# The next head's weights: raw copies in sixteen places instead of eight, their split spread over other slots, and three low parts of eight on GpSimd

## The reference

```python
u = rmsnorm(x, norm_g) @ w_in            # 1024 -> 4096 columns: qa ka va za | qr fr ir zr
# group A, 4 heads: differential attention with a distance bias
scores = einsum(q, k) * SCALE - slope * |q_pos - k_pos|, masked by chunks of 64
a  = softmax(scores[0]) - lam * softmax(scores[1]);  oa = a @ v
# group B, 4 heads: gated linear recurrence over time
state = exp(sum log_f) * state + k^T v;  orec = decayed scores @ v + q exp(cum) @ state
mix = concat(rmsnorm(oa) * silu(za), rmsnorm(orec) * silu(zr))
y   = rmsnorm(x + mix @ w_out, final_g)
# outputs: y, new keys and values, the new states, for both groups
```

## Time and profile before

| | |
|---|---|
| time, median of 3 runs | 1556.78 us (1556.17 to 1558.73) |
| time of the profiled execution | 1557.17 us |
| its span, first to last instruction | 1555.2 us |
| mean granted TensorE clock | 0.992 |
| TensorE, matmuls | 1502.5 us busy (97%) |
| TensorE, weight loads | 1286.8 us (83%) |
| VectorE | 933.1 us (60%) |
| ScalarE | 859.2 us (55%) |
| GpSimd | 678.5 us (44%) |
| chain that ended last | TensorE 84%, VectorE 6%, issue 4%, ScalarE 2%, GpSimd 2% |

### The profile page before, as it was taken

How to read it: one execution, slowest core, us unless ns; L and a number is a source line. 1 busy time by engine, 2 the same in 40 slices (tenths; PEclk the granted TensorE clock), 3 DMA queues, 4 the chain that set the end, 5 groups by cost and what they waited for, 6 DMA issues and landing times.

```text
span 1555.2 us, 25554 instructions
## 1 busy us (share of the span) xinstructions
PE 1502.5 (97%) x8432; PEld 1286.8 (83%) x8432; DVE 933.1 (60%) x2088; ACT 859.2 (55%) x2326; POOL 678.5 (44%) x1407
## 2 busy tenths in 40 slices
PE   5999999998999999989999999989999999899997
PEld 4788888887888888878888888878888888788886
DVE  6676666677555666685556656765656666732232
ACT  5666666756556555665555555755565655621121
POOL 6665555437554444355644444356444334400000
PEclk9999999999999999999999999999999999999999
DMA  7233222243522221133322221234222120434332
GB/s 232 87 128 114 95 79 79 79 146 101 156 72 96 68 68 45 62 119 111 101 90 69 68 69 46 85 97 138 94 68 72 65 69 15 155 127 145 138 121 67
DMA packets 99432, 149.13 MB, mean 96 GB/s; under 512 B 10288, under 2 KB 79792, under 8 KB 90608
## 3 DMA queue, kind: packets, MB, share of 16 engines
q1 hardware_dynamic: 99312, 147.62, 29.2%
HBM read 103.03 MB, written 44.56 MB: 95 GB/s over the span
## 4 chain that ended last, share of the span: by engine, by line
PE 84%; DVE 6%; issue 4%; ACT 2%; POOL 2%; SPq 1%; DMA 1%; DVEq 0%; POOLq 0%; ACTq 0%
PE pab L569 42%; PE oar L641 7%; PE qkb L694 7%; PE qkb L595 6%; PE pab L758 6%; PE qkb L758 6%; PE tb L632 3%; DVE scores L1151 3%; PE tb L673 2%; SPq L305 1%; PE oar L611 1%; PE oar L608 1%; PE tb L533 1%; PE tb L745 1%; PE oar L610 1%
## 5 line engine op out<-in xcount | busy, mean ns | idle before, releaser
L569 PE MATMUL pab<-w_hi,xr 128*128 128x512 f32 x2176 | 783.7, 403 | 5.5 <-DVE w_lo L1030 3.0
L569 PEld LDWEIGHTS pab<-w_hi,xr 128*128 128x128 f32 x2176 | 411.8, 189 | 87.0 <-ACT w_hi L811 4.5
L569 PE MATMUL pab<-w_lo,xr 128*128 128x512 f32 x1088 | 426.7, 392 | 0.0
L1372 POOL TENSOR_TENSOR dd<-dd 128x64 f32<-128x64 f32 x340 | 119.9, 353 | 457.0 <-DVE dd L1136 457.0
L569 PEld LDWEIGHTS pab<-w_lo,xr 128*128 128x128 f32 x1088 | 206.7, 190 | 32.8
L694 PE MATMUL qkb<-kp,q 128*128 128x512 f32 (+3 forms) x656 | 185.1, 364 | 1.8 <-DVE mxs L1151 1.6
L1151 DVE CUSTOM_DVE_ANT_0 scores<-qkb,bias 128x512 f32<-128x512 f32 (+4 forms) x136 | 84.7, 625 | 145.5 <-PE qkb L694 145.4
L914 ACT ACTIVATE scores<-scores,nmx 128x128 f32<-128x128 f32 (+16 forms) x136 | 156.9, 1165 | 19.0 <-DVE nmx L1161 19.0
L859 ACT ACTIVATE fb<-pab 128x256 f32<-128x256 f32 x68 | 26.1, 384 | 255.5 <-PE pab L569 255.5
L641 PE MATMUL oar<-vv,at 128*128 128x128 f32 x1104 | 151.8, 277 | 1.9 <-ACT at L880 1.9
L1106 DVE TENSOR_TENSOR q<-tb,q 128x256 fp32r<-128x256 f32 x68 | 28.9, 425 | 203.4 <-ACT kp L901 203.2
(11 more groups left out here) (151 smaller groups left out, 2624.1 us busy)
## 6 DMA issues: line engine op xcount, KB each, us to landing
xr<-xs SPq DMA_DIRECT2D x51, 1024.0 KB, 5.3
xs<-xr SPq DMA_DIRECT2D x17, 1024.0 KB, 3.9
w_raw<-in_w_in SPq DMA_DIRECT2D x48, 256.0 KB, 5.8
mix<-mx SPq DMA_DIRECT2D x68, 128.0 KB, 2.2
xr<-mix SPq DMA_DIRECT2D x17, 512.0 KB, 5.0
w_raw<-in_x_prompt SPq DMA_DIRECT2D x16, 512.0 KB, 3.9
scores<-in_x_prompt SPq DMA_DIRECT2D x16, 512.0 KB, 4.2
out<-vv SPq DMA_DIRECT2D x16, 512.0 KB, 3.0
```

What stands on the lines that cost most here:

```text
L569: last = mm(pab[:, b, :], x, w[:, kt, 512 * b:512 * b + 512], start=(kt == 0 and part == 0 and w is w_hi), stop=(kt == KT - 1 and part == 1))
L1372: g.tensor_tensor(o[:, :, 0, :], ref, c[:, :, 0, :], sub)
```

## The change

- `w_raw` gets 16 places, one for each piece. The raw weights of `b = 0` of the next head are loaded in slot 5, those of `b = 1` as before; `raw_behind` is gone. The smaller scratch area of the last hunk makes room for it.
- ScalarE splits pieces 0 to 5 of `b = 1` ahead of the last slot's `recurrence_columns`, and 6 and 7 right behind them. The places where pieces of `b = 1` stood now hold pieces 0 to 5 of `b = 0`, and 6 and 7 stand behind `gate_sigmoids`.
- GpSimd makes three low parts of eight in each half, 2, 4 and 6; of `b = 1` it makes two ahead of `exponents`. VectorE makes five instead of six. This also holds for the first head's weights at the start of the kernel.
- In the last slot VectorE's `apply_decay` stands ahead of the biased scores instead of behind them.

```diff
-LO_POOL = (2, 6)
+LO_POOL = (2, 4, 6)
...
-        w_raw = sb("w_raw", [P, 4, 1024])
+        w_raw = sb("w_raw", [P, 8, 1024])
...
-            return w_raw0[kt][:, 512 * b:512 * b + 512] if first else w_halves[:, kt, :]
+            return w_raw0[kt][:, 512 * b:512 * b + 512] if first else w_halves[:, KT * (1 - b) + kt, :]
...                                     # SyncE
-                def raw_ahead(kt):
+                def raw_ahead(b, kt):
                     if not first:
-                        name, n = lo_of(0, kt)
+                        name, n = lo_of(b, kt)
                         need(sp, h, name, n)
                         apart(sp)
-                    raw_load(following, 1, kt)
-                def raw_behind(kt):
-                    name, n = lo_of(1, kt)
-                    need(sp, h + 1, name, n)
-                    apart(sp)
-                    raw_load(following, 0, kt)
+                    raw_load(following, b, kt)
...
                         for kt in range(KT):
-                            raw_ahead(kt)
+                            raw_ahead(1, kt)
+                    if t == 5:
+                        for kt in range(KT):
+                            raw_ahead(0, kt)
...
-                    if t == SAMPLE:
-                        for kt in range(2):
-                            raw_behind(kt)
...
-                        for kt in range(2, KT):
-                            raw_behind(kt)
...                                     # ScalarE, head()
+                    if t == SAMPLE:
+                        split_weights(h, 1, range(6))
                     recurrence_columns(h, t)
+                    if t == SAMPLE:
+                        split_weights(h, 1, (6, 7))
...
-                    if t == SAMPLE:
-                        split_weights(h, 1, (0, 1))
...
-                        split_weights(h, 1, (2, 3))
+                        split_weights(h, 0, (0, 1))
...
-                            split_weights(h, 1, (4 + c,))
+                            split_weights(h, 0, (2 + c,))
...
-                        split_weights(h, 0, range(KT))
+                        split_weights(h, 0, (6, 7))
...                                     # VectorE
-            split_weights(-1, 1, (4, 5, 7))
-            split_weights(-1, 0, (0, 1, 3, 4, 5, 7))
+            split_weights(-1, 1, (5, 7))
+            split_weights(-1, 0, (0, 1, 3, 5, 7))
...
                 chunks = chunks_of(t)
+                if t == SAMPLE:
+                    apply_decay(h, t)
...
-                    apply_decay(h, t)
+                    if t < SAMPLE:
+                        apply_decay(h, t)
...
-                        split_weights(h, 1, (4, 5, 7))
+                        split_weights(h, 1, (5, 7))
...
-                        split_weights(h, 0, (4, 5, 7))
+                        split_weights(h, 0, (5, 7))
...                                     # GpSimd
-            split_weights(-1, 1, (6,))
+            split_weights(-1, 1, (4, 6))
...
-                        split_weights(h, 1, (2,))
+                        split_weights(h, 1, (2, 4))
                     exponents(h, t)
...
-    nc = bacc.Bacc("TRN2", target_bir_lowering=False, num_devices=1)
+    nc = bacc.Bacc("TRN2", target_bir_lowering=False, num_devices=1, dynamic_dma_scratch_size=1024)
```

## The result

| | before | after |
|---|---|---|
| median of 5 runs each, same chip | 1558.63 us (1556.17 to 1558.92) | 1548.09 us (1547.63 to 1549.50) |
| span of the profiled execution | 1555.2 us | 1546.3 us |
| mean granted clock of TensorE | 0.992 | 0.993 |

The ratio is 0.9939, with a 95% interval of 0.9927 to 0.9950: 10.5 us faster. The forecast was 1536, the range 1530 to 1547. The measured time lies outside it, about half of the forecast gain came, and it lies 2 us above the 1546 of rival A.

A forecast was written before the change was run, and what follows sets the result against it. TensorE, busy 97% of the span, was taken as the bound, so only its waits and slow stretches could go: three changes of head at 6.33 us (19.0) plus 1.8 at the last, 20.8 in all, gave 1536 us, range 1530 to 1547.

The forecast's parts named there:

- rival A: GpSimd and VectorE hold each other up, most of the gain goes into a new wait: 1546 us; chance 0.18.
- the attention (a): First transposes to value matmuls, ScalarE's copy behind split pieces: 0.9 of 0.99 us won per change of head.
- the wait (b): TensorE's 0.99 us wait ahead of `b = 0`, `kt = 1`, behind a low part, would go.
- ScalarE's early high parts: Six pieces of `b = 1` fit idle time ahead of `L859`, two ahead of the softmax: cost nothing, otherwise up to 1.07 us.
- the loads: Eight raw load issues move to slot 5: cost 0, at worst what hides nowhere of 7.43 us per head.
- the output projection: The last change, into the output projection: gross gain 2.5 us, 0.7 taken back by GpSimd's late low parts, 1.8 left.
- What is late next: GpSimd: Behind `rec_scores` at each change of head, TensorE waits 1.5 us for GpSimd's first low part of `b = 0`.
- the upper bound of 3.6: That new TensorE wait, in us, if GpSimd also waits for VectorE's three low parts of `b = 0`.
- (d), the slow clock: Clock of 0.50 after the wait ahead of `rec_scores`: 2.14 us per change of head, to go with that wait.
- the 2 us for right and the 3 us for wrong: Sign: TensorE's longest wait for a GpSimd low part is 1 to 2 us if right, above 3 if wrong.
- the early low parts beside tile 15's scores: GpSimd's two early low parts of `b = 1` delay VectorE there: 0.3 us per change, bounds 0 and 1.3.
- the start of the kernel: VectorE loses two low parts and GpSimd gets two: 0, with 0.5 us either way.

The follow-up runs named there:

- x2_loads_only: The kernel before with only sixteen raw places and all raw loads of `b = 0` in slot 5, splits unchanged: 1557.85 us, ratio 1.0000.
- x11_order_only: The changed kernel with GpSimd's three low parts of `b = 1` between tile 15's score maxima and the exponents: 1539.20 us.
- x1_two_low: The changed kernel with two low parts of eight on GpSimd (2, 6) instead of three, six on VectorE, also at the start: 1549.70 us.
- x12_decay_alone: The kernel before with only VectorE's decayed keys of tile 16 moved ahead of the biased scores: 1552.36 us, ratio 0.9970.
- x10_scan_last: The changed kernel with VectorE's cumulative sum of tile 16 behind its low parts 3, 5, 7 of `b = 1`: 1551.81 us.

## Why the prediction was wrong

The steps that held: the chain to the next head's weights is the place; the attention (a) gave 2.65 - 1.80 = 0.85 us of 0.9; the wait (b) is gone; ScalarE's early high parts fit, and the softmax of tile 15 was not late; VectorE reached `L1178` at 684.2 without idle time; the loads cost nothing (`x2_loads_only`; a head has 16 of them, not the "24 + 8" of the prediction, which entered no sum); and the output projection gave 1.7 us of 1.8, though TensorE's wait for a low part in `L726` did not go but turned from 1.2 us for VectorE to 1.6 for GpSimd.

The step that failed is "What is late next: GpSimd", the term 1.5 us. It measured 0.96 + 2.83 = 3.79 us per change, above even the upper bound of 3.6. The walk took the distances of the kernel before as they were, and they were not its own: each depends on what VectorE does beside it. From the end of the exponents (681.91) to the start of the queries (686.04) passed 4.1 us, not 2.5. The low part between took 1.75 instead of 1.30 us, and the three tiny instructions of `head_scales` 2.4 us with their gaps instead of 1.3, since VectorE's low parts of `b = 0` and behind them its decayed keys now lay beside them; in the earlier trace rows the low parts lay beside the queries. And the first of the three low parts took 2.24 us and not 1.245. The walk also overlooked that `rec_scores` itself needs the queries: it forecast no wait there, and the whole lateness in one place behind it. With GpSimd's low parts out of the way (`x11_order_only`), 2.8 us came back over the two slots of the second and of the third change, 1.2 us at the first, where the clock had not fallen, and 1.0 in the last slot.

Of the signs that the prediction had named, `L1178` before 690 us and VectorE without idle time came true; `rec_scores` without a wait and a clock of 1.0 throughout did not. The longest single wait, 2.83 us, lies between the 2 us for right and the 3 us for wrong, so that sign alone would not have told.

Rival A named this mechanism and its time came true, partly by chance: it took both upper bounds in every change. The first, 3.6, was about right. The second, 1.3 us for the early low parts beside tile 15's scores, was 1.2 us, but only once, in the last head's slot; in its place the clock fell.

The second failed term is (d), the slow clock, 2.14 us, which I had counted as won because the wait ahead of `rec_scores` went. I had given the new wait 1.5 us without asking what the clock does behind it. It fell in two of three changes, for 1.6 us each. The size of (d) also differed from change to change in the kernel before, while the prediction took that of the second for all: from `L595` to `L664` pass 5.72, 6.33 and 6.63 us, so (d) was 1.5, 2.1 and 2.4. By the measured terms a second change is 0.85 + 0.99 + 4.10 + 2.14 - 3.79 - 1.6 = 2.7 us, and the table has 2.72.

The third is the start of the kernel, which I had put at 0 with 0.5 either way, since no wait for a low part lay there. With GpSimd's third low part two such waits appear in the first slot, of 0.84 and 0.76 us, both for VectorE; this is the first:

```profile
19.42 0.47 PE L562 MATMUL pab<-w_hi,xr 128*128 128x512 f32 x1 [0.84 <-DVE w_lo L1025]
```

In the profiled executions the start up to the second slot's transposes takes 50.3 to 51.1 us in the four kernels that split the first head's weights as before (`before`, `x1_two_low`, `x2_loads_only`, `x12_decay_alone`) and 52.0 to 54.4 in the ten others.

Of the span of 1555.2 us the forecast wanted 20.8 gone, and 8.9 went. The missing 11.9 are 3 x 2.29 = 6.9 for GpSimd's lateness, 2 x 1.6 = 3.2 for the clock, 0.9 for the start and 0.4 for the early low parts (1.3 once instead of 0.3 three times); some 0.5 is spread over the other terms.

The Trainium skill, "SBUF — State Buffer", section "Who interferes with whom", says that VectorE's two-input instructions and GpSimd's reads exclude one another and that the order of issue decides who blocks. The 1.86 us agree with the first. But the subtraction was released behind the scan's end at 676.27 and ran only when all three low parts of 1.86 us were through. By the order of issue I would estimate about 0.6 us of waiting, for the one low part under way; it did not get its turn then, and the trace decides. Nor is it always so: GpSimd's low part that starts at 681.91, in the midst of three of VectorE's, ends at 683.66, and VectorE's three end at 684.20 only, the last of them after 1.79 us instead of 0.7. There GpSimd got its turn between them. No run here shows what decides it.

What stays open: why the clock fell behind 2.83 us of waiting at the second and third change and not at the first, whose rows are alike; the rest of the median of `x10_scan_last`; and why kernels with the same start differ by up to 2.4 us there.
